# First mixer: all four heads' decay differences taken by VectorE instead of two each by VectorE and ScalarE

## What is computed

```python
acs = jnp.cumsum(dtc * a, axis=1)
seg = acs[:, :, None] - acs[:, None, :]
decay = jnp.exp(jnp.where(causal, seg, -jnp.inf))
cb = jnp.einsum('btgn,bsgn->btsg', cc, bc)
scores = cb[..., None] * decay * dtc[:, None]
y_diag = jnp.einsum('btsgj,bsgjp->btgjp', scores, xc)
y_off = jnp.einsum('btgn,bgjpn->btgjp', cc, state) * jnp.exp(acs)[..., None]
decay_end = jnp.exp(acs[:, -1:] - acs) * dtc
new_state = state * jnp.exp(acs[:, -1])[..., None, None] + jnp.einsum('bsgn,bsgj,bsgjp->bgjpn', bc, decay_end, xc)
```

## Time and profile before

| | |
|---|---|
| median of 3 runs | 3313.91 us |
| all runs | 3313.91, 3313.91, 3308.28 us |
| the profiled execution | 3309.39 us, span 3307.6 us |
| busy in the span | PE 2873.8 us (87%), DVE 2116.9 us (64%), ACT 1469.0 us (44%) |
| the eight groups of the first mixer | from about 92 us to about 397 us of the span |

### The profile page before, as it was taken

The page is one execution under the profiler, slowest core; times in us unless marked ns, Lnnn a source line. Parts: engine busy times, 40 slices in busy tenths (PEclk is TensorE's granted clock), DMA queues, the critical chain, the costliest instruction groups (busy, mean ns, idle before and its releaser), DMA issues.

```text
span 3307.6 us, 36365 instructions
## 1 busy us (share of the span) xinstructions
PE 2873.8 (87%) x12231; PEld 2134.3 (65%) x12231; DVE 2116.9 (64%) x3326; ACT 1469.0 (44%) x2215; POOL 193.0 (6%) x168
## 2 busy tenths in 40 slices
PE   7888899999989899999888887888775988888883
PEld 6666677887868578878564333554344877776772
DVE  4666645777369667762456887431425988888884
ACT  4555443223245542232233453321324877777772
POOL 0000000000000000000000000000001222222221
PEclk9888999999989899999899888989977999999997
DMA  3111222322331023323211000213018999999995
GB/s 104 52 55 53 77 71 83 102 91 71 88 94 52 26 77 101 101 71 95 71 67 48 1 0 17 80 37 110 13 43 292 356 362 362 360 360 360 362 361 164
DMA packets 292139, 437.13 MB, mean 132 GB/s; under 512 B 27371, under 2 KB 172195, under 8 KB 292035
## 3 DMA queue, kind: packets, MB, share of 16 engines
q1 hardware_dynamic: 272163, 363.42, 32.0%
q0 software_dynamic: 19872, 72.36, 8.1%
HBM read 394.84 MB, written 40.89 MB: 132 GB/s over the span
## 4 chain that ended last, share of the span: by engine, by line
PE 60%; SPq 18%; DVE 9%; ACT 4%; DMA 3%; issue 3%; ACTq 0%; POOLq 0%; DVEq 0%; PEldq 0%
PE tp L1001 35%; SPq L773 13%; PE tp L960 5%; SPq L780 4%; PE tp L1054 2%; PE tp L1055 2%; PE tp L1056 2%; PE tp L1316 1%; DMA ytab<-arena 1%; PE mp L1020 1%; PE mp L1034 1%; DVE wring_r L2155 1%; PE tp L1306 1%; DVE wring L2772 1%; PE mp L1231 1%
## 5 line engine op out<-in xcount | busy, mean ns | idle before, releaser
L1001 PE MATMUL tp<-sq_r,arena_r 128*128 128x512 f32 x1152 | 460.2, 399 | 42.5 <-DVE uT_r L2168 25.1
L1001 PE MATMUL tp<-uT_r,arena_r 128*128 128x512 f32 x1152 | 460.9, 400 | 0.0
L1001 PE MATMUL tp<-sq_r,wring_r 128*128 128x512 f32 x1152 | 459.1, 399 | 0.0
L1001 PEld LDWEIGHTS tp<-sq_r,arena_r 128*128 128x128 f32 x1152 | 219.2, 190 | 104.2 <-issue 47.9
L1001 PEld LDWEIGHTS tp<-uT_r,arena_r 128*128 128x128 f32 x1152 | 219.4, 190 | 54.0 <-issue 1.9
L1001 PEld LDWEIGHTS tp<-sq_r,wring_r 128*128 128x128 f32 x1152 | 219.4, 190 | 48.7
L1001 PE MATMUL tp<-arena_r,wring_r 128*128 128x512 f32 x608 | 242.9, 399 | 0.0
L2155 DVE TENSOR_TENSOR wring_r<-wring,arena_r 128x2048 fp32r<-128x2048 f32 x80 | 179.7, 2286 | 79.3 <-ACT arena_r L1581 79.2
L1581 ACT ACTIVATE arena_r<-wring 128x2048 fp32r<-128x2048 f32 x80 | 148.9, 1909 | 56.0 <-DMA wring<-in_w_in 21.9
L1001 PE MATMUL tp<-arena_r,sq_r 128*128 128x512 f32 x480 | 154.7, 404 | 19.6 <-DVE arena_r L2168 19.6
L1568 ACT ACTIVATE raw<-tp 128x512 f32<-128x512 f32 x74 | 44.0, 599 | 261.9 <-PE tp L1001 183.3
(11 more groups left out here) (445 smaller groups left out, 6293.7 us busy)
## 6 DMA issues: line engine op xcount, KB each, us to landing
arena<-in_w_exp_down SPq DMA_DIRECT2D x64, 1024.0 KB
wring<-in_w_exp_gu SPq DMA_DIRECT2D x64, 768.0 KB
uT<-in_w_exp_gu SPq DMA_DIRECT2D x32, 768.0 KB
sq<-in_w_exp_gu SPq DMA_DIRECT2D x32, 768.0 KB
wring<-in_f_up_w SPq DMA_DIRECT2D x22, 1024.0 KB, 5.2
wring<-in_f_up_w SPq DMA_DIRECT2D x44, 512.0 KB, 6.7
wring<-in_w_exp_gu SPq DMA_DIRECT2D x32, 512.0 KB
wring<-in_f_down_w SPq DMA_DIRECT2D x32, 448.0 KB, 5.5
```

The source lines that it names most:

```text
L1001: ins = nc.tensor.matmul(b[:], parts[wp][:, kk, m * P:(m + 1) * P], xparts[xp][:, kk, :], start=n_k == 0 and q == 0, stop=n_k == k - 1 and ...
```

## The change

The two heads that ScalarE handled with Relu go to VectorE. The code of VectorE becomes a function `differences(j)`, called for heads 0 and 1 where it stood before, and for heads 2 and 3 between `group_lo` of quarter 2 and `xdt`. ScalarE takes exp of the rows of heads 2 and 3 and, once VectorE has the differences, exp of these. The semaphore `seg` now counts four per group; `relu` is gone.

```diff
             def group_states(g):
                 pe.wait_ge(ssd["xde"], g + 1)
-                pe.wait_ge(ssd["seg"], 2 * g + 2)
+                pe.wait_ge(ssd["seg"], 4 * g + 2)
...
                 for j in range(2):
-                    act.wait_ge(ssd["seg"], 2 * g + j + 1)
+                    act.wait_ge(ssd["seg"], 4 * g + j + 1)
                     nc.scalar.activation(sg[j], sg[j], ACT.Exp).then_inc(ssd["exped"], 1)
                 for j in (2, 3):
                     act.wait_ge(ssd["rows"], 4 * g + j + 1)
                     nc.scalar.activation(ea[j], mp[j - 2][:], ACT.Exp).then_inc(ssd["ea"], 1)
-                    for c in range(TC):
-                        s = slice(c * P, (c + 1) * P)
-                        ins = nc.scalar.activation(sg[j][:, s], mp[j - 2][:, s], ACT.Relu, scale=-1.0,
-                                                   bias=col(acs, c * HEADS + 4 * g + j))
-                    ins.then_inc(ssd["relu"], 1)
                 for j in (2, 3):
-                    act.wait_ge(ssd["relu"], 2 * g + j - 1)
-                    nc.scalar.activation(sg[j], sg[j], ACT.Exp, scale=-1.0).then_inc(ssd["exped"], 1)
+                    act.wait_ge(ssd["seg"], 4 * g + j + 1)
+                    nc.scalar.activation(sg[j], sg[j], ACT.Exp).then_inc(ssd["exped"], 1)
...
-                for j in range(2):
+                def differences(j):
                     dve.wait_ge(ssd["ea"], 4 * g + j + 1)
                     for c in range(TC):
                         s = slice(c * P, (c + 1) * P)
-                        ins = V.tensor_scalar(sg[j][:, s], mp[2 + j][:, s], col(acs, c * HEADS + 4 * g + j), 0.0,
+                        ins = V.tensor_scalar(sg[j][:, s], mp[(j + 2) % 4][:, s], col(acs, c * HEADS + 4 * g + j), 0.0,
                                               ALU.subtract, ALU.min)
                     ins.then_inc(ssd["seg"], 1)
+
+                for j in range(2):
+                    differences(j)
                 group_lo(n, (2,))
+                for j in (2, 3):
+                    differences(j)
                 per_token(xdt, dtk).then_inc(ssd["xdt"], 1)
```

More of the change, by code:

```diff
@@ L534, in build @@
             "ea",
-            "relu",
             "picked",
```

## The result

| | before | changed |
|---|---|---|
| median of 10 runs each | 3312.41 us | 3319.11 us |
| lowest to highest | 3308.21 to 3314.45 us | 3316.24 to 3325.76 us |
| profiled execution (span) | 3309.39 us (3307.6) | 3318.73 us (3317.0) |

The changed kernel takes 1.0022 times as long, 95% interval 1.0013 to 1.0031: 6.7 us slower, between 4.3 and 10.3 us. The forecast was 3315, with a range of 3309 to 3321, so the time lies in the range; the term that I had summed, 3.3 us, was half of what was measured.

A forecast was written before the change was run, and what follows sets the result against it. The prediction took TensorE to bound each group, waiting for VectorE only at the close. Waits of 2.3 us (group 3) and 1.0 (group 6) sum to 3.3, giving 3312.7 or 3317.2 by run level; it named the middle, 3315, range 3309 to 3321.

The forecast's parts named there:

- the term that I had summed: TensorE's added waits at the close: 2.3 us in group 3, 1.0 in group 6, 0 elsewhere, together 3.3 us.
- The string: VectorE, from `xdt` to the third state: eight more instructions per group, overlapping, make it 2.3 us later (2.1 to 2.4).
- Rival C: VectorE's new instructions run end to end without overlap: 3.0 us per group, together 7.2 us, 3319; chance 0.05.
- ScalarE's relief: ScalarE loses eight Relu, about 2 us per group; counted at nothing because VectorE's own string of work hides it.
- The new wait of ScalarE: ScalarE's exp of the differences of heads 2 and 3 now waits for VectorE; ends about 144.7, needed 147.8: no stall.
- rival D: ScalarE's relief reaches the path through table loads in three groups' openings: up to 3.8 us gained, 3311; chance 0.15.
- Only the close counts: Other work queued behind VectorE's 2.3 us is covered by more than that; only TensorE's close of the group can wait.
- The room: Delay VectorE may take before TensorE waits at the close: 2.49, 2.31, 3.07, 0, 2.44, 2.80, 1.30, 2.54 us, groups 0 to 7.
- a higher clock at their start: Sign against the forecast: TensorE's first close matmul waits in most groups by over 0.5 us.
- rival B: TensorE's clock falls in the new gaps of groups 3 and 6: 6.5 us, up to 8.2, 3318 to 3320; chance 0.12.
- warm starts: Groups happening to start at TensorE's higher clock: a gain up to 3.8 us, limited because VectorE's later string delays the close.
- The chances: Faster 0.05, same 0.78, slower 0.17; the line is 0.2%, 6.6 us: faster below 3307.3, slower above 3320.5.

The follow-up runs named there:

- no_relu: Kernel before with the Relus of heads 2 and 3 left out and their work not added to VectorE (computation incomplete): 3312.51 us, ratio 1.0002 to the kernel before.
- relu_kept: Changed kernel with ScalarE still doing eight Relu of the same size per group, results unused: 3321.31 us, ratio 1.0025 to the kernel before.
- states_first: Changed kernel with each group's four state instructions put ahead of the first half of the convolution on VectorE: 3311.44 us, ratio 0.9994 to the kernel before.
- before_states_first: Kernel before with the states put ahead of the first half of the convolution on VectorE: 3308.47 us, ratio 0.9989 to the kernel before.
- after_shifted: Changed kernel with two extra additions of 512 columns on VectorE just ahead of group 0: 3320.45 us, ratio 1.0028, 6.0 us slower than the kernel before so shifted.
- double_dose: Changed kernel with the eight differences of heads 2 and 3 made a second time on VectorE, into unused tiles: 3335.42 us, ratio 1.0068 to the kernel before.

## Why the prediction was right, and where it was not

**The string, right.** 2.33 us against 2.3, eight instructions at the price of L2313, overlapping as before (2.07 us for eight). Rival C, instructions end to end, did not come: eight records of 0.34 us would make 2.75, and the rows show 2.07 from the first start to the next line. The prediction cited only one half of what the Trainium skill says of it ("VectorE: DVE Perf Modes", section "The DRAIN you can't avoid"): the same paragraph goes on that a next operation which is not held starts earlier. The overlap of these rows agrees with that second half.

**ScalarE's relief at nothing, right.** no_relu shows it: 1.0002. The new wait of ScalarE stalls nothing that is waited for, and what hides it is the idle time before L1651 (54 us in the seven groups that show it). The relief does one thing that the prediction used without giving it a price ("once the Relus are gone"): it sets when VectorE may begin the differences of head 3. By relu_kept that is worth 0.5 to 0.6 us of the string per group. Of rival D nothing came: the table loads in the opening are where they were, as the line of L1670 (L1671 before) in the changed kernel shows:

```profile
L1670 ACT ACT_TABLE_LOAD  x3: 1283/1283/1283, 92.0 to 254.4; - x3
```

The Trainium skill's statement ("ScalarE: Activation LUTs", section "Table sets: the hidden batching unit") that relu is in every table set agrees with this.

**Only the close counts, right in the mixer.** In states_first TensorE waits at no close, and its mixer is no longer than that of before_states_first (304.7 against 305.7 us). By the medians 2.7 us remain between these two, which no profile places.

**The room, wrong.** The sum went over the eight rooms of the earlier trace rows as if they were fixed: 2.3 us in group 3, 1.0 in group 6, nothing in the others. The changed kernel waits 2.67 us in group 1, for which I had 2.31 of room, and nothing in group 3. The rooms are those of one execution and follow from which groups start at 2.4 GHz. The prediction saw this danger in rival D and in its signs ("a higher clock at their start") and gave it no term. That the sum of the waits came out (3.35 against 3.3) is luck, since after_shifted has 6.85 us of them. The prediction also read the earlier trace rows as variation from run to run; those are two groups of one execution. From execution to execution the count went from 61 to 66 in the kernel before, and stayed at 77, group by group, in the changed one.

**The clock term, missing from the sum.** I had weighed two effects of the clock: a fall within the new gap (rival B), and warm starts as a small gain in D. The first did not come: gaps of 2.67 us (changed), 2.99 and 3.08 us (double_dose) leave the close at its 0.44 us records. Where the gap was 3.57 us the close ran at the lower level, 10.27 us from its first matmul to the start of the last of the projection instead of 8.62. TensorE's timeline of group 0 of double_dose:

```profile
120.56 1.14 PE L1110 MATMUL mp<-arena 128*64 128x128 f32 x8 [3.50 <-DVE arena L2333]
121.44 0.69 PE L1112 MATMUL mp<-arena 128*64 128x128 f32 x4
```

In relu_kept, with a gap of 3.27 us in group 3, the matmuls slow down 1.1 us behind the gap, and the stretch is longer by the same 1.65 us. What I did not see was that a later string cannot be had back: a warm start, worth up to 2.4 us on the way to the close (17.9 against 20.3 us in the kernel before), is eaten by the wait after it, while cold starts stay. In the first profiles that was 16 cold matmuls more, 3.2 us, beside the 3.35 of waits. How the 6.7 us of the medians divide is not shown: over the three pairs of profiles the waits alone are 4.5 us and the cold matmuls 1.0. So the sum of the waits was too small, 3.3 against 4.5 in the mean, and the clock term that the sum lacked was 3.2, 2.2 and -2.4 us in the three pairs.

**The chances.** I gave 0.78 to a change within 0.2% and 0.17 to slower. The median is 0.22% slower, just over 0.2%, though below the 3320.5 us that I had reckoned from the first three runs; the interval of 0.13 to 0.31% holds the line. It is slower beyond doubt, and I had named the mechanism as the likeliest case with half its size. The levels between runs that I allowed for by naming the middle (3315) did no harm: with the 3.3 us on the median of ten runs it would have been 3315.7. That the range holds the result is in part luck: its upper end came from rival B, whose fall of the clock in the gap did not happen, and without B's 3.2 us it would have ended at 3317.2.

## What to carry to other kernels

A room read from one profile is a sample: if the engine that hides the added work changes its clock from one execution to the next, ask what the room is in the group where that engine runs fastest, and price every group of the kind at that. Work added to an engine with idle time is safe only behind the instruction that others wait for; moving the nine state instructions ahead of six convolution steps took the waits away and brought the changed kernel to the time of the one before. Make the same move in the kernel before as well: there it gained 3.8 us, so part of what looks like the cost given back is the gain of the move. And look first at the waits on the chain itself: two short ones in the opening were worth about three times the whole change (3308.5 to 3288.9 us).

## What the runs showed of the hardware

In the middle of dense work, idle gaps of TensorE of 2.67, 2.99 and 3.08 us left the matmuls at the pace of 2.4 GHz; the gaps of 3.27 and 3.57 us were each followed by a stretch at 1.2 GHz that cost 1.65 us. Which groups begin at the higher clock repeated exactly in two executions of the changed kernel, differed in two of the kernel before, and differed again with 1.42 us of VectorE work added ahead of the mixer. With two waits of 0.9 and 0.8 us removed from the opening and the states first, seven of eight groups started warm; with the states first alone it was three.
